# Moving the stick-breaking mask onto the scores and the retention gate products ahead of the value projection, in an eight-block Transformer kernel

## What is computed

```python
proj = hn @ w_in          # rq, rk, rv, rg, sq, sk, sv, gr, gs
ret = head_norm(retention(rope(rq), rope(rk) * 128**-0.5, rv)) * silu(rg)     # 4 heads of 128/256
# stick-breaking, 8 heads of 64, per block of 128 queries:
z = q @ k.T / 8;  mask = k_pos < q_pos
log_one_minus = where(mask, log_sigmoid(-z), 0)
suffix = cumsum_from_the_right(log_one_minus) - log_one_minus
A = where(mask, exp(log_sigmoid(z) + suffix), 0);  sb = A @ v
out = (sigmoid(gr) * (ret @ w_ret_o) + sigmoid(gs) * (sb @ w_sb_o)) @ w_out
```

## Time and profile before

| | |
|---|---|
| runs | 1912.83 us median of 3 (1910.91 to 1914.89) |
| profiled execution, span of the trace | 1908.4 us |
| PE busy | 1880.6 us (99%) |
| PE weight loads busy | 1622.1 us (85%) |
| DVE busy | 1300.4 us (68%) |
| ACT busy | 1119.2 us (59%) |
| POOL busy | 330.9 us (17%) |
| first mixer | about 10 to 220 us; second about 400 to 605 us |

### The profile page before, as it was taken

The page is one execution under the profiler, slowest core; times in us unless marked ns, Lnnn a source line. Parts: engine busy times, 40 slices in busy tenths (PEclk is TensorE's granted clock), DMA queues, the critical chain, the costliest instruction groups (busy, mean ns, idle before and its releaser), DMA issues.

```text
span 1908.4 us, 24906 instructions
## 1 busy us (share of the span) xinstructions
PE 1880.6 (99%) x9073; PEld 1622.1 (85%) x9073; DVE 1300.4 (68%) x1919; ACT 1119.2 (59%) x1685; POOL 330.9 (17%) x559
## 2 busy tenths in 40 slices
PE   9999999999999999999999899999999999999999
PEld 7888888888888888888887688888888887788888
DVE  6687776666776776666568775776666578856664
ACT  6486555555866654655466665654555466665552
POOL 1110123111101441022100000431122111101220
PEclk9999999999999999999999999999999999999999
DMA  8866689868657997688865454997788787646884
GB/s 281 245 198 189 202 256 293 266 222 251 194 183 217 288 287 230 189 254 254 237 185 183 133 188 139 285 278 232 229 257 253 213 268 239 202 149 193 253 256 140
DMA packets 283497, 429.97 MB, mean 225 GB/s; under 512 B 25028, under 2 KB 161440, under 8 KB 283120
## 3 DMA queue, kind: packets, MB, share of 16 engines
q1 hardware_dynamic: 256144, 352.41, 59.8%
q0 software_dynamic: 26768, 75.64, 14.6%
q10 hardware_dynamic: 464, 0.34, 0.1%
HBM read 393.15 MB, written 35.15 MB: 224 GB/s over the span
## 4 chain that ended last, share of the span: by engine, by line
PE 86%; DVE 6%; ACT 4%; DMA 2%; issue 1%; POOL 0%; ACTq 0%; DVEq 0%
PE M L955 27%; PE M L957 27%; PE M L956 27%; DVE WL L1479 2%; ACT WH L1217 1%; PE AUX L999 1%; PE AUX L1186 1%; DMA TG<-squares 1%; PE AUX L1164 1%; DMA squares<-TG 1%; DVE SM L1665 1%; ACT TMP L1252 0%; DVE TMP L1622 0%; DMA RAW<-in_w_in 0%; PE AUX L1013 0%
## 5 line engine op out<-in xcount | busy, mean ns | idle before, releaser
L1479 DVE TENSOR_TENSOR WL<-RAW,WH 128x1024 fp32r<-128x1024 f32 (+1 forms) x670 | 810.5, 1215 | 447.9 <-ACT WH L1217 445.8
L1217 ACT ACTIVATE WH<-RAW 128x1024 fp32r<-128x1024 f32 (+1 forms) x670 | 704.1, 1054 | 528.7 <-PE M L957 480.5
L955 PE MATMUL M<-WH,Bh 128*128 128x512 f32 x1792 | 689.2, 385 | 2.0 <-DVE Bl L1506 1.7
L956 PE MATMUL M<-WL,Bh 128*128 128x512 f32 x1792 | 679.9, 379 | 0.0
L957 PE MATMUL M<-WH,Bl 128*128 128x512 f32 x1792 | 679.9, 379 | 0.0
L955 PEld LDWEIGHTS M<-WH,Bh 128*128 128x128 f32 x1792 | 339.2, 189 | 52.2 <-issue 3.2
L957 PEld LDWEIGHTS M<-WH,Bl 128*128 128x128 f32 x1792 | 339.1, 189 | 48.1
L956 PEld LDWEIGHTS M<-WL,Bh 128*128 128x128 f32 x1792 | 339.2, 189 | 45.8
L1247 ACT ACTIVATE AS<-M,KEEP 128x256 f32<-128x256 f32 x132 | 55.3, 470 | 78.3 <-PE M L957 78.2
L955 PE MATMUL M<-WH,MTh 128*128 128x512 f32 x128 | 52.9, 413 | 0.0
L1894 POOL TENSOR_TENSOR KEEP<-SM,KEEP 128x2 f32<-128x2 f32 x15 | 10.6, 710 | 219.9 <-DVE SM L1533 219.9
(11 more groups left out here) (473 smaller groups left out, 2741.4 us busy)
## 6 DMA issues: line engine op xcount, KB each, us to landing
RAW<-in_ffn_w_in SPq DMA_DIRECT2D x352, 256.0 KB, 3.8
RAW<-in_w_in SPq DMA_DIRECT2D x103, 512.0 KB, 4.7
RAW<-in_w_gate_up SPq DMA_DIRECT2D x176, 256.0 KB, 4.4
RAW<-in_ffn_w_out SPq DMA_DIRECT2D x88, 512.0 KB, 4.6
RAW<-in_w_down SPq DMA_DIRECT2D x44, 512.0 KB, 4.7
RAW<-in_x_w_kv SPq DMA_DIRECT2D x32, 512.0 KB, 4.6
RAW<-in_even_w_in SPq DMA_DIRECT2D x24, 512.0 KB, 4.5
RAW<-in_odd_w_in SPq DMA_DIRECT2D x24, 512.0 KB, 5.2
```

Source lines behind the costliest of these rows:

```text
L955: e.matmul(out, s.hi, wh, start=s.at0, stop=False)
L956: e.matmul(out, s.hi, wl, start=False, stop=False)
L1217: e.activation(p.WH[:, h, 0:s.size], p.RAW[:, i, 0:s.size], ACT.Copy).then_inc(k.w_hi, 1)
L1479: e.tensor_tensor(p.WL[:, h, 0:s.size], p.RAW[:, s.u % NRAW, 0:s.size], hi.bitcast(F32), ALU.subtract).then_inc(k.w_lo, 1)
```

## The change

The stick mask is a large negative number that is added once to the raw scores when DVE takes them out of their bank ("st_m", new), over all 384 columns; ACT then works from SBUF, and both later masks go. With masked scores, A is exp(z + the suffix sum that includes the own key), so the triangular matrix counts the diagonal too and log_sigmoid is not formed. The rg chunks stand before sv; Silu is written to temporary tiles; normalisation, products and their transposes ("rgm", new) follow the second rg chunk closely. Planned times shift: rope's transposes 1.6 units earlier, ret_s 2 units later, the first suffix sums 1.7 units earlier. The first stick pair stays where it was on PE's list: 5.5 units before the end of sv, which is 2.5 units after the end of the second rg chunk.

```diff
-    before = (i[:, None] < i[None, :]).astype(np.float32)
-    after = -(i[:, None] > i[None, :]).astype(np.float32)
+    shut = np.where(i[:, None] < i[None, :], 0.0, -2.0 ** 100).astype(np.float32)
+    onward = -(i[:, None] >= i[None, :]).astype(np.float32)
...
         for nm, c0 in (("rq", 0), ("rv", 1024), ("rk", 512), ("sq", 3072), ("rv", 1536), ("sk", 3584),
-                       ("sv", 4096), ("rg", 2048), ("rg", 2560), ("gr", 4608), ("gr", 5120)):
+                       ("rg", 2048), ("rg", 2560), ("sv", 4096), ("gr", 4608), ("gr", 5120)):
...
-    "hq": (0.0, 1.3), "ret_s": (0.0, 0.7), "ret_o": (0.9, 1.5), "rg": (0.0, 0.6), "st_z": (0.7, 1.9), "st_p": (0.0, 0.5),
+    "hq": (0.0, 1.3), "ret_s": (0.0, 0.7), "ret_o": (0.9, 1.5), "st_m": (0.0, 0.0), "st_z": (1.3, 2.3), "st_p": (0.0, 0.5),
...
-            self.heads_out(c.end + 5.0, c.end + 20.0, "rope", s, s.xs, [out[i]], [back[i]], f"{which}{l}", "plain", cols(dst), 1.0)
+            self.heads_out(c.end + 3.4, c.end + 20.0, "rope", s, s.xs, [out[i]], [back[i]], f"{which}{l}", "plain", cols(dst), 1.0)
...
-        e0 = c.end + 21.0
+        e0 = c.end + 23.0
...
-        r = self.rsqrt(e0 + 12.5, rsv, 8, v)
+        gated = []
+        for n in range(2):
+            c = self.chunk(f"rg{l}", B, 0, KD, lab)
+            s = self.evict_x("rg", c, nm)
+            gated.append((s, c))
+        r = self.rsqrt(c.end + 0.6, rsv, 8, v)
         for h in range(4):
-            f = self.add("ret_n", e0 + 13.5 + h)
+            f = self.add("ret_n", c.end + 1.3 + 0.5 * h)
...
+            if h % 2:
+                m = self.add("rgm", c.end + 1.4 + 0.5 * h)
...
+        for n, (m, _) in enumerate(gated):
+            self.split(c.end + 2.6 + n, c.end + 17.0 + 2.0 * n, "rgm", m, m.x, *room[n], A, 4 * n, None, f"ra{l}_", 4 * n)
...
-        e0 = c.end + 10.5
+        e0 = c.end - 5.5
...
-                g = self.add("st_p", b + 3.0)
+                m = self.add("st_m", e0 + 2 * GAP * hp + 0.9 + 0.1 * hh)
+                m.z = z
+                g = self.add("st_p", b + 3.2)
-                q = self.add("st_s", b + (4.9 if i else 6.6))
+                q = self.add("st_s", b + 4.9)
-                q.a = self.add("st_a", q.at + 1.8)
-            o = self.add("st_o", b + (8.5 if hp else 9.0))
+            o = self.add("st_o", b + 7.6)
...
-        for n in range(2):
-            c = self.chunk(f"rg{l}", B, 0, KD, lab)
-            s = self.evict("rg", c, nm)
...
-            self.split(c.end + 1.2, c.end + 15.7, "rg", s, s.x, out, back, A, 4 * n, None, f"ra{l}_", 4 * n)
...
         elif s.kind == "st_z":
...
-            e.wait_ge(k.aux_full[b], s.use)
-            e.activation(lb, aux[:, 0:384], ACT.Abs).then_inc(k.act_chain, 1)
+            e.wait_ge(k.aux_out[b], s.use)
+            e.activation(s.sp, p.TMP[s.x.i][:, 0:384], ACT.Abs).then_inc(k.act_chain, 1)
...
         elif s.kind == "st_z":
...
-            e.scalar_tensor_tensor(out=s.sp, in0=aux[:, 0:384], scalar=0.0, in1=lb, op0=ALU.max, op1=ALU.add).then_inc(k.dve_chain, 1)
...
-            e.tensor_tensor(v, v, mask.unsqueeze(1).to_broadcast([P, 2, P]), ALU.mult).then_inc(k.st_sp, 1)
-            e.scalar_tensor_tensor(out=lb, in0=aux[:, 0:384], scalar=0.0, in1=lb, op0=ALU.min, op1=ALU.subtract).then_inc(k.aux_out[b], 1)
+            e.wait_ge(k.st_lb, s.n)
+            e.scalar_tensor_tensor(out=s.sp, in0=p.TMP[s.x.i][:, 0:384], scalar=0.0, in1=s.sp, op0=ALU.max,
+                                   op1=ALU.add).then_inc(k.st_sp, 1)
+        elif s.kind == "st_m":
...
+            e.wait_ge(k.aux_full[z.bank], z.use)
+            e.tensor_tensor(p.TMP[z.x.i][:, 0:384], p.AUX[z.bank][:, 0:384], p.shut, ALU.add).then_inc(k.aux_out[z.bank], 1)
...
-        elif s.kind == "st_a":
-            e.tensor_tensor(lv, lv, p.before.unsqueeze(1).to_broadcast([P, 2, P]), ALU.mult).then_inc(k.st_prob, 1)
...
-    e.dma_start(p.CC[:, P:4 * P], a["c0"][:, P:4 * P]).then_inc(k.d_c0b, 16)
+    e.dma_start(p.CC[:, P:6 * P], a["c0"][:, P:6 * P]).then_inc(k.d_c0b, 16)
```

More of the change, by code:

```diff
@@ L37, in common_constants @@
     ident = np.eye(P, dtype=np.float32)
-    before = (i[:, None] < i[None, :]).astype(np.float32)
-    after = -(i[:, None] > i[None, :]).astype(np.float32)
-    return np.ascontiguousarray(np.concatenate([ident, before, after, -np.ones((P, P), np.float32)], axis=1))
+    shut = np.where(i[:, None] < i[None, :], 0.0, -2.0 ** 100).astype(np.float32)
+    onward = -(i[:, None] >= i[None, :]).astype(np.float32)
+    return np.ascontiguousarray(np.concatenate([ident, shut, shut, 0.0 * ident, onward, -np.ones((P, P), np.float32)], axis=1))
 def first_constants():
@@ L217 @@
 }
-HELD = {"turn": 1.6, "tq": 1.0, "ret_s": 1.2, "ret_o": 1.2, "st_z": 3.0, "st_s": 1.5, "df_s": 3.0, "hg_s": 3.5,
+HELD = {"turn": 1.6, "tq": 1.0, "ret_s": 1.2, "ret_o": 1.2, "st_z": 2.0, "st_s": 1.5, "df_s": 3.0, "hg_s": 3.5,
         "cx_s": 2.5}
@@ L886, in __init__ @@
         self.merged, self.rh_made, self.ret_made = sem("merged"), sem("rh"), sem("ret_n")
-        self.st_lb, self.st_sp, self.st_hi, self.st_lo, self.st_exp, self.st_prob = (
-            sem(x) for x in ("st_lb", "st_sp", "st_hi", "st_lo", "st_exp", "st_prob"))
+        self.st_lb, self.st_sp, self.st_hi, self.st_lo, self.st_exp = (
+            sem(x) for x in ("st_lb", "st_sp", "st_hi", "st_lo", "st_exp"))
         self.unr_made = sem("unr")
@@ L1064, in tensor @@
                 e.wait_ge(k.aux_out[b], s.use - 1)
-            below, nones = p.UNR[:, 0:P], p.UNR[:, P:2 * P]
+            onward, nones = p.UNR[:, 0:P], p.UNR[:, P:2 * P]
             sh, sl = s.p.sh, s.p.sl
-            e.matmul(aux[:, 0:384], below, sh, start=True, stop=False)
-            e.matmul(aux[:, 0:384], below, sl, start=False, stop=False)
+            e.matmul(aux[:, 0:384], onward, sh, start=True, stop=False)
+            e.matmul(aux[:, 0:384], onward, sl, start=False, stop=False)
             e.matmul(aux[:, 256:384], nones, sh[:, 128:256], start=False, stop=False)
@@ L1075, in tensor @@
                 e.wait_ge(k.m_out[sv.c.banks[1]], sv.c.use[1])
-            e.wait_ge(k.st_prob, s.ss[1].a.n)
+            e.wait_ge(k.st_exp, s.ss[1].n)
             if s.use > 1:
@@ L1235, in scalar @@
             for t in range(T):
-                e.activation(halves(s.silu[t]), banks[t], ACT.Silu, scale=r[t]).then_inc(k.m_out[c.banks[t]], 1)
+                vacant(e, k, s.xs[t])
+                e.activation(halves(p.TMP[s.xs[t].i]), banks[t], ACT.Silu, scale=r[t]).then_inc(k.m_out[c.banks[t]], 1)
         elif s.kind == "tanh":
@@ L1342, in scalar @@
             e.wait_ge(k.d_c0b, 16)
-            e.activation(p.UNR[:, :], p.CC[:, 2 * P:4 * P], ACT.Copy).then_inc(k.unr_made, 1)
+            e.activation(p.UNR[:, :], p.CC[:, 4 * P:6 * P], ACT.Copy).then_inc(k.unr_made, 1)
         elif s.kind == "st_z":
@@ L1347, in scalar @@
                 e.preload_act_table_set(LOG_EXP)
-            vacant(e, k, s.x)
-            lb = p.TMP[s.x.i][:, 0:384]
-            e.wait_ge(k.aux_full[b], s.use)
-            e.activation(lb, aux[:, 0:384], ACT.Abs).then_inc(k.act_chain, 1)
+            e.wait_ge(k.aux_out[b], s.use)
+            if s.n > 2:
+                e.wait_ge(k.st_lo, s.n - 2)
+            e.activation(s.sp, p.TMP[s.x.i][:, 0:384], ACT.Abs).then_inc(k.act_chain, 1)
             chain += 1
             e.wait_ge(k.act_chain, chain)
-            e.activation(lb, lb, ACT.Exp, scale=-1.0).then_inc(k.act_chain, 1)
+            e.activation(s.sp, s.sp, ACT.Exp, scale=-1.0).then_inc(k.act_chain, 1)
             chain += 1
             e.wait_ge(k.act_chain, chain)
-            e.activation(lb, lb, ACT.Ln, bias=1.0).then_inc(k.st_lb, 1)
+            e.activation(s.sp, s.sp, ACT.Ln, bias=1.0).then_inc(k.st_lb, 1)
         elif s.kind == "st_p":
@@ L1363, in scalar @@
         elif s.kind == "st_s":
-            lb = p.TMP[s.z.x.i][:, 0:384]
+            if table != "l":
+                table = "l"
+                e.preload_act_table_set(LOG_EXP)
+            x = p.TMP[s.z.x.i][:, 0:384]
             e.wait_ge(k.aux_out[b], s.use)
-            e.activation(lb, lb, ACT.Exp).then_inc(k.st_exp, 1)
+            e.activation(x, x, ACT.Exp).then_inc(k.st_exp, 1)
         elif s.kind in ("st_o", "hg_o"):
@@ L1557, in vector @@
                 e.wait_ge(k.d_mem[m.n - 1][s.kt_half], 32)
-            elif s.source == "rg":
+            elif s.source == "rgm":
                 e.wait_ge(k.rx_made, m.n)
@@ L2031, in build_program @@
         p.RAW = sb("RAW", [P, NRAW, UC], side="right")
-        p.CC = sb("CC", [P, 4 * P], side="right")
-        p.ident, p.before = p.CC[:, 0:P], p.CC[:, P:2 * P]
+        p.CC = sb("CC", [P, 6 * P], side="right")
+        p.ident, p.shut = p.CC[:, 0:P], p.CC[:, P:4 * P]
         p.SM = sb("SM", [P, 640], side="right")
```

39 lines of the change are left out of this document (16 added, 23 removed).

## The result

| | before | after |
|---|---|---|
| median of the runs | 1911.87 us (4 runs, 1910.51 to 1914.89) | 1921.15 us (4 runs, 1920.21 to 1922.52) |
| span of the profiled execution | 1908.4 us | 1918.5 us |
| time of that execution | not shown apart | 1920.34 us |

The ratio is 1.0054, with a 95% interval of 1.0040 to 1.0069: slower by 9.3 us, where the sum said 9.4. The kernel does less and takes longer: on its page (engine, busy us, share, instructions) DVE and ACT have fallen by 10.6 and 12.0 us against the earlier trace rows, and PE is as busy as it was.

The account below looks back on a forecast made before the run. PE, busy for 1880.6 of 1908.4 us, was taken as the bound. 13.4 + 3.4 - 4.0 - 3.4 + 0 = +9.4 us on the span, the median 4.4 above it: 1922.2 us, range 1911 to 1930.

Parts of the forecast that it names:

- The queue on DVE: DVE's work ahead of each layer's first suffix sums: PE loses 6.7 us per layer, +13.4 us in both.
- position 17.4: Earliest start of the first suffix sums, in us after the second rg chunk's end; PE, unhindered, would arrive at 10.7.
- the wait at SK: PE ahead of the first st_z, until ACT copies SK: 2.1 us per layer, counted inside the 6.7.
- Clock: PE's slow clock after the new standstills: one fall per layer, 2 x 1.7 = +3.4 us, between 0 and 6.8.
- Retention wait: PE's wait ahead of layer 0's first retention scores goes, with its slow clock: -4.0 us, between 0 and -4.0.
- Waits at 1067: PE's waits for the softplus's low part ahead of suffix sums, both layers: -3.4 of a possible -5.0 us.
- st_o now follows the Exp closely: Stick outputs planned 0.9 to 1.4 units earlier; named among reasons to take -3.4 of the possible -5.0 us.
- Ropes and mask together: The gains at the first retention scores (-4.0 us) and at the suffix sums (-3.4 us), 7.4 by the terms.
- That the queue is short enough: Rival at the first suffix sums: DVE's work fits into 8.3 us, nothing lost; 1903.8 or 1905.4 us, chance 0.15.
- That the clock falls at both waits: Rival: clock falls at both waits of each layer, later pairs keep their waits; +16.2 us, 1929, chance 0.13.
- Half of it: Rival: first head late by only some 4 us per layer, clock stays up; 1912 us, no difference, chance 0.10.
- the retention wait did go: Contradicts the rival that rk's transfers land no earlier, keeping the first retention scores' wait: 4.0 us more, 1926, chance 0.07.

Follow-up runs that it names:

- half_products: The changed kernel without the gate product of token tile 0, two of four product instructions per layer; 1916.94 us, ratio 1.0033 to the kernel before.
- sk_first: The changed kernel with the variance step planned at 0.8 instead of 0.6 units, behind the copy of SK; 1925.74 us, ratio 1.0074 to the kernel before.
- spread: norm_early with the second product and its transposes behind the first head's low part and the first pair's st_m earlier; 1905.66 us, ratio 0.9968 to the kernel before.
- rope_only: The kernel before with only rope's transposes at 3.4 instead of 5.0 and retention scores at 23 instead of 21 units; 1909.56 us, ratio 0.9991.
- spread_rope: spread with rope's transposes at 5.0 instead of 3.4 units, the retention scores staying at 23; 1911.10 us, ratio 1.0000 to the kernel before.
- rope_back: The changed kernel with rope's transposes back at 5.0 and the retention scores at 21 units; 1923.36 us, ratio 1.0063 to the kernel before.
- mask_only: The kernel before with only the change's stick part (masks, triangle, st_m, stick times), order of rg and sv and gate kept; 1911.67 us, ratio 1.0000.
- after_again: The changed kernel run once more, nothing altered; 1922.59 us, ratio 1.0065 to the kernel before.
- first_late: The changed kernel with each layer's first suffix sums planned at 6.6 units again instead of 4.9; 1917.51 us, ratio 1.0033 to the kernel before.
- norm_early: The changed kernel with normalisation and first product back at their old time, only the second product behind the second rg chunk; 1910.61 us, ratio 0.9995 to the kernel before.

## Why the prediction was right, and where its terms were off

- **The queue on DVE, +13.4.** The list of durations is right to the digit: suffix sums at position 17.4 (119.65 - 102.25 = 17.4), SK at 5.2 where 5.3 was said, PE idle for 1.9 + 4.5 in layer 0, and no wait of PE at the second head, which started at 128.20, position 25.9, where 24.2 was said and 1.7 us of slow clock lie between. The charge made from it was too high: I set 6.7 us per layer against a PE without any wait, though 0.3 of it, by the starts, stood in the kernel before, as the prediction itself says. PE's idle time at the two places rose by 8.9 + 3.5 = 12.4 us. half_products shows the mechanism (1.3 us less work, 1.2 us less wait), sk_first that the wait at SK lies inside it (gone, and the time did not fall), spread its size together with the clock (16.4 us, give or take 3.5, against 16.8).
- **Clock, +3.4.** 4.1 in the profile, with one fall per layer as charged, but a longer one in layer 1 and partly hidden in the wait. The bounds of 0 to 6.8 held.
- **Retention wait, -4.0.** The wait went, in the changed kernel and in rope_only: the transposes of rk start at 50.67 instead of 53.63 and KT is copied from 68.30 (I had said that by 68.3 it would be done). spread_rope shows that the later scores alone remove it. The size failed outside the one profile that I read: 1.7 us in rope_only and 1.7 in rope_back. I took the wait of one execution with its slow stretch for that of all, which the runs do not bear out; in rope_back the same wait had no slow stretch, and in mask_only it was 0.8 us in two. For the span that I worked from, the term was right.
- **Waits at 1067, -3.4.** In the changed kernel they are gone (its suffix sums have a median of 342 ns, those of the earlier trace rows 439). New waits of 1.1 us at the outputs stand against it, so the net is between -2.4 and -3.9, and for the changed kernel the term held; the step "st_o now follows the Exp closely" was named and lay in the 1.6 us that I did not take. By itself the mask is worth nothing that the runs can tell: mask_only measured 0 (give or take 1.9 us), with 2.0 us of waits gone at the suffix sums and 1.6 come at the outputs.
- **Not priced:** two waits for a conversion early in layer 0, once of 0.6 us at 32.09 and 0.9 us in all. My expectation for rope_back laid them to rope's transposes, which pass a conversion. The runs do not bear that out: after_again and first_late have the same transposes and rope_only too, and none has such a wait, and the kernel before has one of 0.3. It is something that differs between executions.
- **Ropes and mask together:** 7.4 by my terms, 6.1 in spread (4.2 to 8.0 by the interval), 1.7 and 0 singly. spread also has the third part, the rg chunks ahead of sv, and no run has ropes and mask without it; so whether the parts add, or the third makes the difference, is not shown.
- **What lies around the span.** I took the median of 1912.8 to be 4.4 us above the span because so much lies around it. In every execution with both numbers the time is only 1.75 to 1.88 us above the span; the profiled execution of the kernel before was simply a fast one, 1908.4 + 1.8 = 1910.2. By my own sum its profile after would have belonged to a time of 1919.6, not 1922.2.
- **Luck.** That 9.3 was measured for 9.4 is closer than the terms deserve. In the profile the queue was 1.0 less than charged and the clock 0.7 more, 1.7 us of short waits came that I had not counted apart, the retention term fits the one execution that I had read, and the two spans differ by 10.1.
- **The rivals.** That the queue is short enough (1903.8 or 1905.4) is what spread had to be rebuilt for, 1905.7. That the clock falls at both waits (1929) did not come; after_again shows why a fall at the first wait can cost nothing. "Half of it" (4 us per layer) is excluded by 6.4 us of waits in each, and the retention wait did go. The plain miss was in an expectation, norm_early: 1906 said, 1910.6 measured, because I took 1.3 us off for transposes in whose time DVE would have waited for ACT anyway.

## What to carry to other kernels

When work is moved ahead on an engine that is 68% busy, add up what stands in its in-order queue between the input and the result that the bound engine waits for; the average share says nothing about that stretch, and a hand-written list of durations foretold it within 0.1 us. Leave out of the list what runs while the engine would wait for another one anyway: taking that away gives nothing (norm_early). Independent work (normalisations, gates, transposes whose result is due 15 us later) belongs behind the first steps of the new chain, not ahead of them: the same instructions in that order were 16 us faster. And the waits that one profile shows are a bound, not a gain: those worth 4.0 us in one trace were worth about 1.7 in the medians, since the slow clock behind them does not always come, and those worth up to 5.0 gave nothing when removed alone, since others came at the next step.

## What the runs showed of the hardware that I had not expected

**A standstill costs clock in one execution and not in the next.** The same wait of about 2.5 us, ahead of a value matmul in the last blocks, left the clock at 1.00 in the kernel before (the stretch from 1628) and in the first profile of the changed kernel. In its second profile, after_again, it did not:

```profile
1640.00:1650.00 10.00, 7.49 (x31) 5.81 (x31) 6.16 (x10) 3.56 (x6) 0.00 (x0) 0.83 0.48 150
```

Nor did it in these two, whose instructions there are the same. In spread:

```profile
1628.00:1640.00 12.00, 10.73 (x46) 9.01 (x47) 4.64 (x9) 7.17 (x12) 0.00 (x0) 0.86 0.43 132
```

and in norm_early:

```profile
1625.00:1640.00 15.00, 11.44 (x52) 8.96 (x51) 11.98 (x24) 7.58 (x12) 0.00 (x0) 0.89 0.40 140
```

All three come to 3.3 or 3.4 us at 1.2 GHz. The other way round, half_products waited 3.3 us in layer 0 and kept its clock behind it:

```profile
118.00:124.00 6.00, 5.80 (x35) 4.94 (x36) 4.22 (x8) 5.17 (x9) 4.01 (x8) 1.00 0.97 256
```

The spread of the kernel before goes with it: of its 63 runs beside the experiments, the 16 with a mean granted clock of 1.000 have a median of 1909.1 us, the 8 with 0.997 one of 1913.7. That the wait for KT comes and goes as well is what I suppose; the runs without a profile don't show it.
